# A merged attention stage: order of TensorE's work within a step, and the prompt mix in column quarters

## The reference, cut to what matters

```
s = einsum('bqhd,bkhd->bhqk', q, k) * scale      # 16 heads of 64
s = s + cq[..., None] - ck[:, :, None, :]        # cumulative log forget values
s = where(k_pos <= q_pos, s, -1e30)
o = einsum('bhqk,bkhd->bqhd', softmax(s), v)
```

## Time and profile before

| | us |
|---|---|
| median of 3 runs | 1935.96 (1932.44 to 1938.0) |
| the profiled execution | 1932.09, span 1930.3 |
| PE busy | 1859.9 (96%) |
| DVE, ACT, POOL busy | 925.4, 693.0, 586.0 |

### The profile page before, as it was taken

One profiled execution on the slowest core, in us unless ns is written; L12 is line 12 of the kernel. 1 busy time (PEld: TensorE's weight loads), 2 busy tenths in 40 slices (PEclk: granted clock), 3 DMA queues, 4 the chain that ended last, 5 costly groups with the idle time before them and its releaser, 6 DMA issues. The chain is left out here.

```text
span 1930.3 us, 40486 instructions
## 1 busy us (share of the span) xinstructions
PE 1859.9 (96%) x16865; PEld 1681.9 (87%) x16865; DVE 925.4 (48%) x1398; ACT 693.0 (36%) x1090; POOL 586.0 (30%) x296
## 2 busy tenths in 40 slices
PE   6999998999999999999997999999989999999998
PEld 5999997999999999998994666665659999999998
DVE  4757767245555511146543555555542555555000
ACT  5365454432122222156523544444443312222111
POOL 2333332233333433234321111111103333334332
PEclk9999999999999999999998999999989999999999
DMA  5232231222223232242438999898873322223322
GB/s 121 79 101 80 81 110 50 77 83 82 87 78 88 85 91 76 72 145 51 144 114 312 313 339 337 329 337 331 322 289 116 88 79 86 82 83 89 91 76 79
DMA packets 289098, 273.70 MB, mean 142 GB/s; under 512 B 19602, under 2 KB 250099, under 8 KB 288404
## 3 DMA queue, kind: packets, MB, share of 16 engines
q1 hardware_dynamic: 286980, 268.62, 43.1%
q10 hardware_dynamic: 1792, 1.44, 0.3%
q0 software_dynamic: 144, 1.05, 0.1%
HBM read 254.64 MB, written 16.43 MB: 140 GB/s over the span
## 5 line engine op out<-in xcount | busy, mean ns | idle before, releaser
L1959 POOL TENSOR_TENSOR a_wl<-a_wraw,a_wh 128x1024 fp32r<-128x1024 f32 (+2 forms) x91 | 233.1, 2562 | 395.2 <-ACT a_wh L1883 395.2
L1959 POOL TENSOR_TENSOR b_wl<-b_wraw,b_wh 128x1024 fp32r<-128x1024 f32 (+1 forms) x67 | 175.3, 2617 | 296.3 <-ACT b_wh L1883 296.3
L1840 PE MATMUL ps<-xh,a_wh 128*128 128x288 f32 x1104 | 239.1, 298 | 4.8 <-POOL a_wl L1959 4.8
L1840 PE MATMUL ps<-xl,a_wh 128*128 128x288 f32 x1104 | 237.6, 297 | 0.0
L1840 PE MATMUL ps<-xh,a_wl 128*128 128x288 f32 x1104 | 237.2, 297 | 0.0
L1883 ACT ACTIVATE a_wh<-a_wraw 128x1024 fp32r<-128x1024 f32 (+2 forms) x91 | 100.6, 1105 | 339.5 <-PE ps L1840 324.4
L1883 ACT ACTIVATE b_wh<-b_wraw 128x1024 fp32r<-128x1024 f32 (+1 forms) x67 | 76.0, 1135 | 318.5 <-PE ps L1840 318.5
L1840 PEld LDWEIGHTS ps<-xh,a_wh 128*128 128x128 f32 x1104 | 177.6, 188 | 6.2 <-issue 5.3
L1840 PEld LDWEIGHTS ps<-xl,a_wh 128*128 128x128 f32 x1104 | 177.9, 188 | 0.6
L1840 PEld LDWEIGHTS ps<-xh,a_wl 128*128 128x128 f32 x1104 | 177.7, 188 | 0.6
L1976 DVE TENSOR_TENSOR xT<-xT,ps 128x576 f32<-128x576 f32 x32 | 24.2, 755 | 320.8 <-PE ps L1840 320.8
(11 more groups left out here) (352 smaller groups left out, 3952.7 us busy)
## 6 DMA issues: line engine op xcount, KB each, us to landing
a_wraw<-in_w_gate_up SPq DMA_DIRECT2D x44, 512.0 KB, 3.9
b_wraw<-in_w_gate_up SPq DMA_DIRECT2D x44, 512.0 KB, 3.9
xT<-in_cache_k SPq DMA_DIRECT2D x40, 512.0 KB, 5.4
xT<-in_cache_v SPq DMA_DIRECT2D x40, 512.0 KB, 6.0
a_wraw<-in_a_w_in SPq DMA_DIRECT2D x32, 512.0 KB, 4.2
f_h_plain<-in_cache_k SPq DMA_DIRECT2D x30, 512.0 KB, 5.8
xl_plain<-in_cache_k SPq DMA_DIRECT2D x30, 512.0 KB, 5.9
f_h_plain<-in_cache_v SPq DMA_DIRECT2D x30, 512.0 KB, 5.8
```

What stands on the lines that cost most here:

```text
L1840: mm = pe.matmul(ps[0:width(n), bank(n) + a, 0:HALF], wt[:, base(n) + t, 0:width(n)], ap[:, first + t, a * HALF:(a + 1) * HALF], start=kin ...
L1959: pool.tensor_tensor(part(wl, n), part(wraw, n), part(wh, n).bitcast(F32), ALU.subtract).then_inc(e["low"], 1)
```

## The change

Within a step, PE now does all that uses full columns first: K, T, probabilities, pick, U, tail; then S, M and the prompt mix. The ring's order follows (tail after pick). On ACT the save moves to the end of the step, on DVE the tail moves behind `finish`. The prompt mix is split into four products of 32 columns instead of two of 64, and comes three steps after its first block instead of four; the output copy (`OUT_LAG`) comes one step earlier as well.

```diff
-    TURN_LAG, MIX_LAG, OUT_LAG = 2, 4, 11
+    TURN_LAG, MIX_LAG, OUT_LAG = 2, 3, 10
...
-                    for a in range(2):
-                        mm = pe.matmul(ps[DH * a:DH * (a + 1), OUT_BANK, i * P:(i + 1) * P],
-                                       vrows[:, c, (2 * j + a) * DH:(2 * j + a + 1) * DH], upt[:, a, c * P:(c + 1) * P],
-                                       start=c == 0, stop=c == i, skip_group_check=True)
+                    for q in range(4):
+                        mm = pe.matmul(ps[tile(q), OUT_BANK, i * P:(i + 1) * P], vrows[:, c, 2 * j * DH + TILE * q:2 * j * DH + TILE * (q + 1)],
+                                       upt[:, q // 2, c * P:(c + 1) * P], start=c == 0, stop=c == i, skip_group_check=True)
...
                     key(n, 0)
                     key(n, 1)
-                if 1 <= n <= KSTEPS:
-                    scores(n - 1)
-                if mix_at(n) is not None:
-                    unit_mix(mix_at(n))
                 if unit_at(n, TURN_LAG) is not None:
                     unit_turn(unit_at(n, TURN_LAG))
-                if n < KSTEPS and n % PAGES == 12:
-                    tail(n // PAGES)
...
-                for m in pages.mixed_at(n):
-                    mix(m)
                 for c in range(NB):
                     if n == out_step(c):
                         pick(c)
                 if unit_at(n, 0) is not None:
                     unit_score(unit_at(n, 0))
+                if n < KSTEPS and n % PAGES == 12:
+                    tail(n // PAGES)
+                if 1 <= n <= KSTEPS:
+                    scores(n - 1)
+                for m in pages.mixed_at(n):
+                    mix(m)
+                if mix_at(n) is not None:
+                    unit_mix(mix_at(n))
...
         @block.scalar
-                if n % 4 == 0 and 4 <= n <= KSTEPS:
-                    save(n // 4 - 1)
...
                 if i == U + 1 and 0 <= j < KD - 1:
                     query_high(j + 1)
+                if n % 4 == 0 and 4 <= n <= KSTEPS:
+                    save(n // 4 - 1)
...
         @block.vector
-                if n < KSTEPS and n % PAGES == 12:
-                    tail(n // PAGES)
...
                     if n == out_step(c):
                         finish(c)
+                if n < KSTEPS and n % PAGES == 12:
+                    tail(n // PAGES)
```

More of the change, by code:

```diff
@@ L1089, in attention @@
             enter(("unit", w), "act" if w % 2 == 0 else "dve")
-        if n < KSTEPS and n % PAGES == 12:
-            enter(("tail", n // PAGES), "dve")
         for c in range(NB):
@@ L1101, in attention @@
                 enter(("pick", c), "dve")
+        if n < KSTEPS and n % PAGES == 12:
+            enter(("tail", n // PAGES), "dve")
     def wait_copied(eng, n):
```

## The result

| us | before | after |
|---|---|---|
| median (runs) | 1934.2 (1930.7 to 1938.0) | 1964.2 (1962.6 to 1967.7) |
| profiled execution | 1932.1 | 1967.7 |
| attention, first K to the next trunk's first product | 424.0 | 453.9 |

The change made the kernel slower: the ratio to before is 1.0157, with a 95% interval of 1.0132 to 1.0183. The forecast was 1957, the range 1942 to 1973. The spans differ by 35.5 us, but 5.6 of that is there before the first K (1024.63 against 1019.05), where no code differs. The granted clock does differ there: 0.89, 0.94 and 0.93 in three stretches of 50 us (from 300, 350 and 900) against 0.95, 0.99 and 0.97. Attention itself is 29.9 us longer, as much as the medians.

A forecast was written before the change was run, and what follows sets the result against it. The prediction took PE to bound the attention stage, with transfers following it. Its terms, -11.2 - 5.1 - 8.7 + 46 = +21 us, added to 1936 gave 1957 us, range 1942 to 1973.

The forecast's parts named there:

- Round trips gone: PE in attention steps: one trip between full columns and quarters instead of two, 0.26 us each, 11.2 us saved.
- Prompt mix: PE's prompt mix in quarters behind the value mix: 5.1 us saved, nothing added for doubling the products.
- New waits of U: PE reaches block scores before ACT's exponential is done: 21 us in plain block steps, 17.4 in nine sample-exponential steps.
- Waits at the probabilities: PE in 13 steps: probability transposes reach the key banks before ACT and DVE have copied them, 5.5 us lost.
- Old waits gone: PE's former waits at the block's scores in the key steps disappear into the new ones: 8.7 us.
- The last mix of a head: PE's last prompt mix per head, one step earlier, waits for DVE's copy of the turn: 2 us lost.
- After the last key step: After key step 127, less cover for PE's wait but DVE free earlier: 0, between -1 and +3 us.
- The clock: Rival: long PE waits in attention pull the clock down, nine falls cost 15 us, giving 1972; chance 0.12.
- The fast one: Rival: saved trips win and PE's block scores do not wait for ACT, 25 us go, giving 1911; chance 0.08.
- DMA as the pace: Rival: DMA sets attention's pace, so gains and waits are absorbed and time stays 1936; chance 0.08.

The follow-up runs named there:

- before_exp_first: Kernel before with only ACT's order changed, the block's exponential first in the step: 1921.3 us, ratio 0.9925.
- exp_first: Kernel after with the block's exponential first in ACT's step, ahead of the key copy and the sample's exponentials: 1914.6 us, ratio 0.9893 to before.
- sample_exp_late: Kernel after with the sample's exponentials moved behind the block's exponential on ACT: 1940.1 us, ratio 1.0032 to before.
- before_quarters: Kernel before with only the prompt mix in four products of 32 columns, at its old place: 1931.0 us, ratio 0.9978.
- u_before_prob: exp_first plus DVE's copy of the turn right behind its key copy, and block scores ahead of the probability transposes on PE: 1908.0 us, ratio 0.9859.
- before_save_last: Kernel before with only the save moved to the end of ACT's step: 1926.8 us, ratio 0.9973.

## Why the prediction was right, step by step

The profiled executions repeat so closely, step by step, that the sum can be redone from the start of K in step 20 to its start in step 127:

| kernel | us |
|---|---|
| before | 340.3 |
| before_exp_first | 332.2 |
| exp_first | 326.0 |
| sample_exp_late | 350.6 |
| after | 369.6 |

| term | forecast | these traces |
|---|---|---|
| waits of U in the kernel after (after less exp_first, less the clock) | 21 + 17.4 | 35.8 |
| half clock in the key steps (after against sample_exp_late, above) | 0 | 7.7 |
| old waits of U gone (before less before_exp_first) | -8.7 | -8.1 |
| trips, prompt mix, waits at the probabilities and at the last mix (before_exp_first less exp_first) | -11.2 - 5.1 + 5.5 + 2 | -6.2 |
| before step 20 | 0 | -1.3 |
| after the last K | 0 | +2.0 |
| sum | +21 | +29.9 |

So without the clock the traces give 22, and the forecast said 21. That these two are so close is partly luck: the waits of U were put 2.6 us too high, and what the trips and the mix leave was put 2.6 us too high as well. The time came out at 1964.2 instead of 1957 because the sum lacks 9 us, most of it the clock, and was added to 1936, where before now has 1934.2. The first term also holds what little exp_first changes in the steps with probabilities.

- *Round trips gone (11.2 us).* The starts are as forecast: T right behind K, S 0.46 before M. That the gain is real is shown by exp_first, which has all of the change and almost none of U's waits and is 7 us below before_exp_first. The full 11 was not measured by itself: the mix's 5.1 and the new waits at the probabilities and at the last mix lie in the same 7. Forecast for the four together was 8.8 us, measured 6.2.
- *Prompt mix (5.1 us, nothing for the products).* Sizes held: 32 instructions take 1.01 us and end the step, after 0.63 us of wait for DVE's copy, which the sum had for this step:

```profile
1104.35 0.61 PE L1316 MATMUL ps<-at_pages,at_pp 128*32 128x256 f32 x8
1105.60 1.08 PE L1369 MATMUL ps<-at_upt,f_l_plain 128*32 128x128 f32 x32 [0.63 <-DVE at_upt L1626]
1106.61 0.33 PE L1253 MATMUL ps<-ident,f_l_plain 128*128 128x128 f32 x1
```

 before_quarters gave 3 us (3.6 by its trace) where 2.6 was worked out for its place.
- *New waits of U (21 + 17.4 us).* The mechanism is shown twice. Moving U away from the wait, or moving the exponential, takes the wait away, and the time with it. The size: plain steps have 1.69 to 2.01 from K to U, where 1.66 to 1.95 and the 0.05 of K behind M had been worked out, and the long ones 2.8 to 3.3. The profile's idle time is smaller than the waits by starts (0.59 against 0.76 in the step above), as it counts from the modelled end of PE's last product; so the idle times of the key steps add up to 30.4 us (33.6 less the 3.2 after them), and the steps to 35.8.
- *Waits at the probabilities (5.5).* The size fits: u_before_prob regained 4.0 us in the key steps by covering most of them.
- *Old waits gone (8.7).* before_exp_first shows 13, of which 8.1 in the key steps. ACT's save was 4.8 of them, as before_save_last shows.
- *The last mix of a head (2).* In two steps the mix starts 1.25 us after M instead of 0.43, as above, where DVE's group maximum stands ahead of the copy; in three others it starts 0.2 us late. That makes 2.2 us.
- *After the last key step (0, -1 to +3).* It was 39.1 us against 37.1, from the last key step's K on: +2. U's wait there grew from 2.4 to 3.2 us.
- *The clock (rival, 0.12).* This is the term that was mis-sized. The forecast held none of it, the rival all nine falls and 15 us. There were five in the key steps, which held back 10.2 us of clock (half of the time at half clock, by stretches of 2 us); it cost 7.7 us, as part of it fell where U would have waited anyway or PE idled (that reason is argued). In the kernel before, the key steps had none. The clock was lower in all four executions of the kernel after, 0.981 to 0.983 on average over the whole kernel, where those of before have 0.985 to 0.993.
- *Rivals.* The fast one would have needed ACT's chain ready when PE arrives; it becomes true in exp_first, by ACT's order, and there the sign does turn. DMA as the pace is refuted: its share fell from 0.90 to 0.84 and SP's waits for PE grew.

## What to carry to other kernels

An order that is good for one engine can put a waiting instruction in front of the work that used to hide its wait. Before grouping instructions, follow each one's releaser back to what starts that chain, measure the distance from there, and compare it with where the instruction will stand. If it is too short, look first at the releaser's own queue: here the same grouping lost 30 us with the exponential behind the key copy, and gained 7 with it in front (before_exp_first against exp_first). The exponential's move alone, without any grouping, gained 13.

## What was not expected of the hardware

PE's clock fell to half after a single idle of 1.73 us between busy steps (1171.79), while 38 idles of 0.55 us on average in another run cost none of it. And 32 instructions in the array's quarters took 0.87 us where 16 in its halves had taken 1.02 with the change of mode around them. The 0.87 is 4 x 0.21 us of streaming and little more: the number of instructions did not show in the time.
